# Output projection in eight PSUM banks, splits of the merged sums shared out anew, high halves moved, and layer-norm sums made elementwise

## What is computed

```python
proj = rms_norm(x) @ w_in
# branches a (HGRN2), b (mLSTM), c (short conv), d (Conformer conv), 512 wide each
glu = ad * sigmoid(gd); y_d = causal_depthwise_conv(glu, 31 taps)
o_d = silu(layer_norm(y_d + bias))         # mean and mean square over 512 channels
merged = sum_i sigmoid(gate_i) * (branch_i @ w_branch_i)
x = x + merged @ w_out
x = x + square(relu(rms_norm(x) @ w_up)) @ w_down     # 4096 wide
```

## Time and profile before

| | |
|---|---|
| runs | 2362.89, 2359.77, 2351.19 us; median 2359.77 |
| profiled execution | 2358.25 us, its span 2356.5 |
| TensorE matmuls busy | 2300.2 us (98%) |
| VectorE, ScalarE, GpSimd busy | 934.1, 555.9, 791.4 us |
| chain that ended last | TensorE 92%, VectorE 4%, issue 2%, DMA 1% |
| granted TensorE clock, mean | 0.993 of full speed |

### The profile page before, as it was taken

The page is one execution under the profiler, slowest core; times in us unless marked ns, Lnnn a source line. Parts: engine busy times, 40 slices in busy tenths (PEclk is TensorE's granted clock), DMA queues, the critical chain, the costliest instruction groups (busy, mean ns, idle before and its releaser), DMA issues.

```text
span 2356.5 us, 33198 instructions
## 1 busy us (share of the span) xinstructions
PE 2300.2 (98%) x13490; PEld 2166.8 (92%) x13490; DVE 934.1 (40%) x1431; ACT 555.9 (24%) x915; POOL 791.4 (34%) x528
## 2 busy tenths in 40 slices
PE   6999999999999999999999998999999999999998
PEld 5999998999998999999999998779989899898896
DVE  5389744534543353002122124462342432423324
ACT  4333231111142122121121212132212122121232
POOL 4577433232221124232132313234324233242341
PEclk9999999999999999999999999999999999999999
DMA  4112220120135557212112121201111111111112
GB/s 147 39 37 73 68 78 24 56 57 22 45 93 75 75 68 110 83 45 83 45 45 83 45 83 56 81 18 54 38 49 40 45 45 45 45 45 45 45 54 76
DMA packets 176797, 139.00 MB, mean 59 GB/s; under 512 B 14637, under 2 KB 155197, under 8 KB 176673
## 3 DMA queue, kind: packets, MB, share of 16 engines
q1 hardware_dynamic: 174197, 127.83, 22.0%
q0 software_dynamic: 2304, 8.91, 0.9%
q10 hardware_dynamic: 180, 0.59, 0.1%
HBM read 118.94 MB, written 18.73 MB: 58 GB/s over the span
## 4 chain that ended last, share of the span: by engine, by line
PE 92%; DVE 4%; issue 2%; DMA 1%; POOL 1%; ACT 1%; SPq 0%; POOLq 0%; DVEq 0%; ACTq 0%
PE acc L689 28%; PE acc L691 28%; PE acc L690 28%; PE pz L805 2%; DVE proj_a L1673 1%; DMA branch_outputs<-gb 1%; DVE h_lo L1673 1%; PE acc L718 0%; PE acc L719 0%; PE pz L854 0%; DVE full L1673 0%; PE acc L715 0%; PE acc L716 0%; PE pz L947 0%; PE pz L825 0%
## 5 line engine op out<-in xcount | busy, mean ns | idle before, releaser
L689 PE MATMUL acc<-h_hi,w_hi 128*128 128x368 f32 (+1 forms) x2616 | 864.8, 331 | 6.9 <-ACT kqr L1064 4.7
L691 PE MATMUL acc<-h_hi,w_lo 128*128 128x368 f32 (+1 forms) x2616 | 858.2, 328 | 0.0
L690 PE MATMUL acc<-h_lo,w_hi 128*128 128x368 f32 (+1 forms) x2616 | 857.0, 328 | 0.0
L1401 POOL TENSOR_TENSOR w_lo<-w_raw,w_hi 128x1024 fp32r<-128x1024 f32 (+1 forms) x169 | 405.6, 2401 | 898.1 <-ACT w_hi L1064 863.1
L689 PEld LDWEIGHTS acc<-h_hi,w_hi 128*128 128x128 f32 x2616 | 493.1, 188 | 13.2 <-issue 11.4
L690 PEld LDWEIGHTS acc<-h_lo,w_hi 128*128 128x128 f32 x2616 | 493.3, 189 | 0.3
L691 PEld LDWEIGHTS acc<-h_hi,w_lo 128*128 128x128 f32 x2616 | 493.2, 189 | 0.0
L1064 ACT ACTIVATE w_hi<-w_raw 128x1024 fp32r<-128x1024 f32 (+1 forms) x169 | 176.4, 1044 | 548.1 <-PE acc L691 510.2
L1673 DVE TENSOR_TENSOR x<-acc,x 128x512 f32<-128x512 f32 x315 | 217.8, 691 | 209.6 <-PE acc L691 200.5
L691 PE MATMUL acc<-w_hi,u_lo 128*128 128x512 f32 x480 | 190.2, 396 | 0.0
L689 PE MATMUL acc<-w_hi,u_hi 128*128 128x512 f32 x480 | 189.2, 394 | 0.3 <-POOL w_lo L1401 0.3
(11 more groups left out here) (341 smaller groups left out, 2686.1 us busy)
## 6 DMA issues: line engine op xcount, KB each, us to landing
w_raw<-in_w_in SPq DMA_DIRECT2D x84, 512.0 KB, 3.8
w_raw<-in_w_up SPq DMA_DIRECT2D x32, 512.0 KB, 4.0
w_raw<-in_w_down SPq DMA_DIRECT2D x32, 512.0 KB, 3.7
b_raw<-branch_outputs POOLq DMA_DIRECT2D x16, 544.0 KB, 7.3
w_raw<-in_w_branch SPq DMA_DIRECT2D x16, 512.0 KB, 3.6
xin<-in_x_prompt SPq DMA_DIRECT2D x8, 512.0 KB, 7.2
x<-in_x_prompt SPq DMA_DIRECT2D x16, 256.0 KB, 5.2
w_raw<-in_w_out SPq DMA_DIRECT2D x8, 512.0 KB, 3.7
```

The lines of the kernel that those rows point to most:

```text
L689: pe.matmul(out, lh, rh, start=first, stop=False)
L690: pe.matmul(out, lh, rl, start=False, stop=False)
L691: return pe.matmul(out, ll, rh, start=False, stop=last)
L1401: return pool.tensor_tensor(out, x, y, op)
```

## The change

- **Norm sums.** The four `y_d` tiles are added first (VectorE 0+1, GpSimd 2+3, VectorE both), so that one tile goes through the matrix of ones; the same for the four squares, which now lie in four tiles (`ln_t`, `ln_r`, `sg_d`, `y_c`). Places in the list: sum 3, mean 12, centre 14, squares 17, 18, 20, 21, sum 23, var 32, root 33, reciprocals 35 to 38, scales 39 to 42, gates 41 to 47, store 49 and 52 (before: 4, 6, ..., 48 and 51).
- **Splits of merged.** GpSimd takes tiles 0, 1, 2 in the list and 4, 6 after the second projection weight's split; VectorE takes 3, 5, 7 behind the first, third and fifth group that it adds in part 0 of the projection. ScalarE makes the samples' low parts as copies out of `h_lo` (`sample_low`), and no longer waits for "br" groups in `evac`.
- **Projection, first half.** Group e (0 to 35) uses bank `e % 8` of all eight (`pz` first); TensorE waits for the add of group e-8, and each part for the splits that it reads.
- **Memory.** `u_hi` lies next to `u_lo`; `m_s` has its own place above `merged`; `ur`, `uu`, `gfin`, `junk1` move.

The diff, with most of the context and blank lines left out:

```diff
@@ -181,10 +181,11 @@
...
     first = value("ia", 0) + heads(a_names, 0)
-    norm = [(4, "mean", 0), (6, "centre", 0)] + [(at, "square", t) for t, at in enumerate((9, 10, 15, 18))] + \
-           [(at, "var", t) for t, at in enumerate((14, 17, 20, 23))] + [(26, "root", 0)] + \
-           [(28 + 2 * j, "invert", j) for j in range(4)] + [(36 + t, "scale", t) for t in range(FT)] + \
-           [(40 + 2 * t, "gate", t) for t in range(FT)] + [(48, "store", 0), (51, "stored", 0)]
+    norm = [(3, "sum", 0), (12, "mean", 0), (14, "centre", 0)] + \
+           [(at, "square", t) for t, at in enumerate((17, 18, 20, 21))] + \
+           [(23, "sum", 1), (32, "var", 0), (33, "root", 0)] + \
+           [(35 + j, "invert", j) for j in range(4)] + [(39 + t, "scale", t) for t in range(FT)] + \
+           [(41 + 2 * t, "gate", t) for t in range(FT)] + [(49, "store", 0), (52, "stored", 0)]
     first = [item for item in first if item[0] == "half"]
@@ -260,7 +261,7 @@
...
 O_U, O_B, O_G = NU, FILLS[-1], GROUPS[-1]
-O_UN, O_BN, O_GN = 8, 15, 45
+O_UN, O_BN, O_GN = 8, 3, 45
@@ -416,19 +417,20 @@
...
             u_lo = sb(st, "u_lo", [P, FT, TP], F32R)
+            u_hi = sb(st, "u_hi", [P, FT, TP], F32R)
             u_s = sb(st, "u_s", [P, FT, 2 * TS], F32R)
-            ur = sb(st, "ur", [P, 2, 368])
-            uu = sb(st, "uu", [P, 2, 368])
-            gfin = sb(st, "gfin", [P, 2, 512])
-            junk1 = sb(st, "junk1", [P, 2, 2, 512])
             with ExitStack() as norm_only:
...
             w_x = sb(st, "w_x", [P, 2, 2, UNIT], F32R)
+            ur = sb(st, "ur", [P, 2, 368])
+            with ExitStack() as merge_only:
+                m_s = sb(merge_only, "m_s", [P, KT, 2 * TS], F32R)
+            uu = sb(st, "uu", [P, 2, 368])
             sb(st, "pad_l", [P, 288])
-            u_hi = sb(st, "u_hi", [P, FT, TP], F32R)
-            m_s = u_hi[:, 0, :].rearrange("p (k n) -> p k n", k=KT)
+            gfin = sb(st, "gfin", [P, 2, 512])
+            junk1 = sb(st, "junk1", [P, 2, 2, 512])
             spill_o = gfin[0:TS]
@@ -493,6 +495,10 @@
...
                     END_U + 4: END_G, END_U + 5: END_G, END_U + 6: END_G + 9, END_U + 7: END_G + 12}[u]
+        def o_bank(e):
+            return pz[:, e % 8, :] if e % 8 < 5 else acc[:, e % 8 - 5, :]
@@ -941,19 +947,15 @@
...
                         pe.wait_ge(sem("tails_done"), 2)
-                        pe.wait_ge(sem("conv_done"), FT)
-                        for k in range(FT):
-                            for j, (c0, c1) in enumerate(cuts):
-                                mm = pe.matmul(pz[:, j, 0:c1 - c0], ones, y_d[:, k, c0:c1], start=k == 0,
-                                               stop=k == FT - 1)
+                        pe.wait_ge(sem("ln_added"), 3)
+                        for j, (c0, c1) in enumerate(cuts):
+                            mm = pe.matmul(pz[:, j, 0:c1 - c0], ones, ln_t[:, c0:c1], start=True, stop=True)
                         mm.then_inc(sem("ln_sum"), 1)
                     elif stage == "var":
-                        if t == 0:
-                            pe.wait_ge(sem("ln_dve"), FT)
-                        pe.wait_ge(sem("ln_act"), t + 1)
+                        pe.wait_ge(sem("ln_dve"), FT)
+                        pe.wait_ge(sem("ln_added"), 6)
                         for j, (c0, c1) in enumerate(cuts):
-                            mm = pe.matmul(pz[:, j, 0:c1 - c0], ones, (ln_t, ln_r)[t % 2][:, c0:c1], start=t == 0,
-                                           stop=t == FT - 1)
+                            mm = pe.matmul(pz[:, j, 0:c1 - c0], ones, ln_t[:, c0:c1], start=True, stop=True)
                         mm.then_inc(sem("ln_sum"), 1)
@@ -971,14 +973,20 @@
...
                 pe.wait_ge(w_ready, O_U + 1 + s)
-                pe.wait_ge(sem("merged_low_a"), s + 1)
-                pe.wait_ge(sem("merged_low_b"), s + 1)
+                pe.wait_ge(sem("merged_low_b"), s + 2)
+                if s:
+                    pe.wait_ge(sem("merged_low_a"), s)
+                else:
+                    pe.wait_ge(sem("b_gated"), H)
                 for n, c in enumerate(ORDER):
+                    e = 9 * s + n
+                    if e >= 8:
+                        pe.wait_ge(sem("o_added"), e - 7)
+                    elif e >= 5:
+                        pe.wait_ge(acc_free[e - 5], O_B)
                     if c == NT:
                         pe.wait_ge(sem("m_s_ready"), s + 1)
-                    pe.wait_ge(acc_free[n % 3], O_B + 3 * s + n // 3)
-                    wide_mm(acc[0:max(rows_of[c], P), n % 3, :], [(O_U + s, 2 * s)], c, h_hi, h_lo, m_s) \
-                        .then_inc(group_ready, 1)
+                    wide_mm(o_bank(e), [(O_U + s, 2 * s)], c, h_hi, h_lo, m_s).then_inc(group_ready, 1)
@@ -993,7 +1001,10 @@
...
             for n, c in enumerate(ORDER):
-                pe.wait_ge(acc_free[n % 3], O_B + 12 + n // 3)
+                if n < 3:
+                    pe.wait_ge(sem("o_added"), 30 + n)
+                else:
+                    pe.wait_ge(acc_free[n % 3], O_B + n // 3)
                 if n == 0:
@@ -1114,6 +1125,8 @@
...
                 kind, name, idx = UNITS[u]
+                if kind == "br":
+                    return
                 act.wait_ge(group_ready, GROUPS[u] + g + 1)
@@ -1198,6 +1211,13 @@
...
+            def sample_low(s):
+                act.wait_ge(sem("merged_low_b"), s + 2)
+                if s:
+                    act.wait_ge(sem("merged_low_a"), s)
+                copy(m_s[:, 2 * s:2 * s + 2, TS:], h_lo[:, 2 * s:2 * s + 2, TP:T].bitcast(F32)) \
+                    .then_inc(sem("m_s_ready"), 1)
             for it in ITEMS:
@@ -1225,9 +1245,7 @@
...
                         act.wait_ge(sem("ln_dve"), t + 1)
-                        if t >= 2:
-                            act.wait_ge(sem("ln_sum"), t)
-                        act.activation((ln_t, ln_r)[t % 2][:, :], y_d[:, t, :], ACT.Square) \
+                        act.activation((ln_t, ln_r, sg_d, y_c)[t][:, :], y_d[:, t, :], ACT.Square) \
                             .then_inc(sem("ln_act"), 1)
@@ -1255,7 +1273,9 @@
...
                     if k % 2:
-                        copy(m_s[:, k - 1:k + 1, 0:TS], merged[:, k - 1:k + 1, TP:T]).then_inc(sem("m_s_high"), 1)
+                        copy(m_s[:, k - 1:k + 1, 0:TS], merged[:, k - 1:k + 1, TP:T])
+                    if k == 5:
+                        sample_low(0)
                 elif it[0] == "rows":
@@ -1303,6 +1323,9 @@
...
                 wide_hi(O_U + j)
+                if j == 1:
+                    for s in range(1, 4):
+                        sample_low(s)
             act.wait_ge(sem("o_added"), 27 + PLACE[NT] + 1)
@@ -1477,6 +1500,11 @@
...
+            def merged_low(k):
+                pool.wait_ge(sem("mh_ready"), k + 1)
+                tt(h_lo[:, k, :], merged[:, k, :], h_hi[:, k, :].bitcast(F32), ALU.subtract) \
+                    .then_inc(sem("merged_low_b"), 1)
             for it in ITEMS:
@@ -1520,16 +1548,19 @@
...
                     _, stage, t = it
-                    if stage == "scale":
+                    if stage == "sum" and t == 0:
+                        pool.wait_ge(sem("conv_done"), FT)
+                        tt(ln_r[:, :], y_d[:, 2, :], y_d[:, 3, :], ALU.add).then_inc(sem("ln_added"), 1)
+                    elif stage == "sum":
+                        pool.wait_ge(sem("ln_act"), 4)
+                        tt(sg_d[:, :], sg_d[:, :], y_c[:, :], ALU.add).then_inc(sem("ln_added"), 1)
+                    elif stage == "scale":
                         pool.wait_ge(sem("ln_dve"), FT + 6 + t)
...
                             .then_inc(sem("ln_affine"), 1)
-                elif it[0] == "msplit" and it[1] % 2 == 0:
-                    k = it[1]
-                    pool.wait_ge(sem("mh_ready"), k + 1)
-                    tt(h_lo[:, k, :], merged[:, k, :], h_hi[:, k, :].bitcast(F32), ALU.subtract) \
-                        .then_inc(sem("merged_low_b"), 1)
+                elif it[0] == "msplit" and it[1] < 3:
+                    merged_low(it[1])
                 elif it[0] == "bload":
@@ -1607,7 +1638,10 @@
...
-            for j in range(1, 8):
+            wide_lo(O_U + 1)
+            merged_low(4)
+            merged_low(6)
+            for j in range(2, 8):
                 wide_lo(O_U + j)
@@ -2082,7 +2116,14 @@
...
                     cuts = ((0, 512), (512, 1024), (1024, T))
-                    if stage == "centre":
+                    if stage == "sum":
+                        x, y, z = (y_d[:, 0, :], y_d[:, 1, :], ln_r[:, :]) if t == 0 else \
+                            (ln_t[:, :], ln_r[:, :], sg_d[:, :])
+                        dve.wait_ge(*((sem("conv_done"), FT) if t == 0 else (sem("ln_act"), 2)))
+                        tt(ln_t[:, :], x, y, ALU.add).then_inc(sem("ln_added"), 1)
+                        dve.wait_ge(sem("ln_added"), 3 * t + 2)
```

(22 more changed lines are left out.)

## The result

The changed kernel takes **2327.6 us** (median of four runs, 2325.97 to 2329.46) against 2359.7 for the kernel before on the same chip, which is a ratio of 0.9868 with a 95% interval of 0.9855 to 0.9881. The profiled execution took 2327.79 us, 30.5 less than the one before.

A forecast was written before the change was run, and what follows sets the result against it. TensorE was taken as the bound, its matmuls filling 98% of the span. From the profiled 2358.25 us, 7.3 (norm) and 13.7 (merge) were subtracted, memory moves 0: 2337.2, given as 2337, range 2329 to 2344.

The forecast's parts named there:

- Norm part: Norm stage: fewer sum matmuls and less standing gain 13.1 us; less costs of 0.2, 3.4 and 2.2, 7.3 us.
- The stall on `va`: Norm's second sum: VectorE's held add delays an evacuation, so TensorE waits 3.4 us near 302; bounds 0 and 6.
- its clock: Lower TensorE clock around the new norm stall: 2.2 us of full-rate work lost, bounds 0 and 3.4.
- The first sum: Norm stage: the mean's adds end at 288.4, TensorE asks at 288.3; cost about 0.2 us.
- the same stall might cost no clock in one run: Norm stall: the clock change depends on a free-running monitor's phase, so the clock loss could be nothing; lower bound 0.
- The lock of VectorE and GpSimd: Norm's second sum: SBUF operations of both engines serialize for whole instructions; if shared, stall 2.1 us, total 1.3 lower.
- The rival without a stall: Norm's second sum is hidden too, with neither stall nor low clock: 2331.6 us; chance 0.15.
- Merge part: Merged splits and output projection: three TensorE waits and the low clock behind them go, gaining 13.7 us; bounds 0 and 13.7.
- The rival in which the wait moves into the projection: Projection: held adds or a late tile 1 stop TensorE 3 us; merge part gives 8 to 9, 2342; chance 0.15.
- Memory moves: Moved buffers change no instruction and address seems not to matter: cost 0, bound plus or minus 1 us.
- u_hi's new place: MLP down steps, 1664 matmuls: reads at the lower address might be slower; at 10%, 2375 us; chance 0.02.
- MLP spacing other than 0.228: Sign that the forecast is wrong: MLP matmuls spaced at something other than 0.228 us.

The follow-up runs named there:

- b1: The kernel before with nothing but the new memory layout: 2350.15 us, ratio 0.9963; its stretch from the `otb` to the `xt` wait takes 679.01 us.
- f1: The changed kernel with the second norm sum at list place 27 instead of 23 and the last scale at 43 instead of 42: 2323.67 us, ratio 0.9853.
- n2: The changed kernel with only the second norm sum moved, to list place 27 instead of 23: 2327.15 us, ratio 0.9865.

## Why the forecast was wrong

**Norm part: right, with luck in the last digit.** 7.3 us were forecast, 7.2 measured at the first landmark; over the traces with the old and the new norm list it is anything from 5.8 to 9.1, 9.1 being against the trace whose clock did not fall. The stall on `va` was 2.9 (3.4), its clock 1.7 in this execution (2.2), the records six and 2.04 us each as said. The first sum, forecast to cost 0.2, cost nothing: its add ends at 287.85, and its matmuls start at 288.78 right behind the products. Two waits that had no term took that place: the 0.54 us for ScalarE's evacuation at 284.36, and the 0.99 us for `w_lo` at 339.09, from the scalings moved as a block ahead of a weight split on GpSimd. Together the costs were forecast at 5.8 us and measured 6.1. The forecast also said that the same stall might cost no clock in one run, and that no single trace can show it; the two traces of the unedited changed kernel show it, with 1.7 and with nothing. The lock of VectorE and GpSimd was as stated by the Trainium skill ("SBUF — State Buffer", Who interferes with whom) and as the rows said: two-input operations in SBUF were serialized, 2.75 and 3.56 us for 1.29 and 2.53. The rival without a stall (2331.6) got the nearest number, by a wrong reason: its stall was there, 2.89 us.

**Merge part: right.** 13.7 forecast, 13.8 measured (12.4 against b1's stretch), no wait and a clock of 1.00 over 40 us. VectorE's tiles 3, 5 and 7 ended at 1456.2, 1460.4 and 1463.9; the forecast, which counts from the kernel before's start of the stage 7.8 us later, had 1464.2, 1468.3 and 1472.0. The rival in which the wait moves into the projection did not come.

**Memory moves: wrong.** The step that failed is "address seems not to matter. Cost 0; bound plus or minus 1 us." It is worth 7.9 us between the landmarks and, at 5.8 ns, another 1.0 for the 168 such matmuls behind them: 8.9 of the 9.4 us between the sum of 2337.2 and the profiled 2327.79. The two rows that it rested on the earlier trace rows held the answer: 389 ns with `h_lo`, 396 with `u_lo`, for the same 512 columns. I took 7 ns in 396 for sameness. It is 1.8%, and over the 1536 matmuls with these tiles (512 of each kind) it was the whole effect. The row was also harder to read than it looks: `u_lo` starts at a multiple of 256 itself, and its row was slow because of `u_hi`, the tile of the matmul behind it, as the runs with `u_lo` unmoved show (396 ns before, 389 after). The rival "u_hi's new place" had named the right tiles, counted them (its 1664 are these 1536 and 128 for the samples) and priced them, with 38 us for 10%, but only as a loss; that they might be slow now and become normal was not asked. With the term at 5 to 7 ns x 1536 = 7.7 to 10.8 us the sum would have been 2326 to 2330.

Of what would show it, the last item did: "MLP spacing other than 0.228". Before, it was 0.233 (three in 0.70), after 0.227.

## What to carry to other kernels

When one matmul shape has two mean durations in a kernel, ask what differs before calling them equal: 1.5 per cent on a ninth of all matmuls (1536 of 13490) outweighed the norm's whole part. Let stationary fp32r tiles like these (128 x 128) start at multiples of 256 bytes in their partition, and look at their offsets again when a tile ahead of them is resized; other types and shapes were not tried. Count VectorE's and GpSimd's two-input operations in SBUF as one queue, and let the evacuation that TensorE waits for stand ahead of the sum, not behind it: f1 does that, and moves one scaling behind the weight split, with two numbers of a list, and is 4 us faster than the changed kernel. The first of the two alone (n2) showed no gain clear of its spread. And before a difference of a few us between two traces is explained, look at a second trace of the same kernel.

## What was not expected of the hardware

- The start of a stationary fp32r tile costs time: 128 bytes off a multiple of 256 makes an MLP of 708.6 us one of 716.7, 64 bytes off 714.2. The duration changes in the matmul beside the unaligned tile too (`w_hi,u_lo` 396 ns beside an unaligned `u_hi`, 389 otherwise, with `u_lo` unmoved). The height in the partition made no difference over 155,904 to 192,512. For operands of the branch products no such gain was seen.
- The same wait does not always cost the same clock. Behind a stall of 2.88 or 2.89 us in the same place, eleven traces lost nothing, 1.7 or 3.4 us of full-rate work; behind the `proj_a` wait of 2.3 us they lost nothing, 1.7 or 3.4. Two traces of one and the same kernel reach the `proj_a` wait at 363.96 and 362.12.
- Over the runs of the changed kernel's variants the `kqr` wait, behind which stands SyncE's wait for a store to land (`branch_outputs<-gb`, 10.2 us in the changed kernel), was anything from 3.0 to 5.2 us.
